# FF2 weight sums made in earlier stages and kept in HBM; 18 weight octets by seven products instead of 12

## The reference, cut to what matters

```python
x = x + jnp.einsum("bsd,de->bse", mixed, w_out[l])
h = _rmsnorm(x, ln2_w[l])
u = jax.nn.relu(jnp.einsum("bsd,df->bsf", h, w_ff1[l]))       # FF1: 256x2048 by 2048x8192
x = x + jnp.einsum("bsf,fd->bsd", jnp.square(u), w_ff2[l])    # FF2: 256x8192 by 8192x2048
```

## Time and profile before

| | value |
|---|---|
| median of the runs | 1516.24 us |
| profiled execution, its own time | 1515.4 us |
| its span | 1513.7 us |
| PE busy | 1503.6 us (99%), granted clock 1.0 all through |
| DVE busy | 1074.2 us (71%) |
| ACT busy | 783.6 us (52%) |
| GpSimd busy | 85.1 us (6%) |
| moved by DMA | 276.13 MB, mean 182 GB/s |

### The profile page before, as it was taken

The page is one execution under the profiler, slowest core; times in us unless marked ns, Lnnn a source line. Parts: engine busy times, 40 slices in busy tenths (PEclk is TensorE's granted clock), DMA queues, the critical chain, the costliest instruction groups (busy, mean ns, idle before and its releaser), DMA issues.

```text
span 1513.7 us, 19520 instructions
## 1 busy us (share of the span) xinstructions
PE 1503.6 (99%) x7508; PEld 1268.1 (84%) x7508; DVE 1074.2 (71%) x1274; ACT 783.6 (52%) x884; POOL 85.1 (6%) x121
## 2 busy tenths in 40 slices
PE   9999999999999999999999999999999999999999
PEld 6888888888888888888888888888888888888887
DVE  6866645778776877876655556688887566688976
ACT  6555444676654444544344545455544445455543
POOL 5000000000040100100000101100000101100000
PEclk9999999999999999999999999999999999999999
DMA  8565554454544444445655666656666665656662
GB/s 289 183 207 183 184 190 154 153 164 161 174 142 166 140 139 160 141 143 176 241 194 169 196 192 194 189 190 204 204 197 208 187 184 189 193 193 211 208 213 92
DMA packets 140295, 276.13 MB, mean 182 GB/s; under 512 B 7105, under 2 KB 7617, under 8 KB 139969
## 3 DMA queue, kind: packets, MB, share of 16 engines
q1 hardware_dynamic: 138960, 273.05, 55.0%
q10 hardware_dynamic: 1264, 2.13, 0.4%
HBM read 273.06 MB, written 2.10 MB: 182 GB/s over the span
## 4 chain that ended last, share of the span: by engine, by line
PE 95%; DVE 3%; issue 1%; ACT 0%; DMA 0%; SPq 0%; DVEq 0%; ACTq 0%
PE banks L493 43%; PE banks L852 16%; PE banks L920 14%; PE banks L855 8%; PE banks L898 8%; PE banks L509 2%; DVE lo L1404 1%; PE banks L758 1%; PE banks L633 1%; PE banks L606 1%; DVE diag L1423 1%; PE banks L749 1%; DMA x_tok<-in_x 0%; DVE both__111 L1423 0%; ACT hi L953 0%
## 5 line engine op out<-in xcount | busy, mean ns | idle before, releaser
L1404 DVE TENSOR_TENSOR lo<-raw,hi 128x1024 fp32r<-128x1024 f32 x384 | 472.6, 1235 | 317.3 <-ACT hi L953 313.9
L953 ACT ACTIVATE hi<-raw 128x1024 fp32r<-128x1024 f32 x383 | 404.7, 1058 | 439.6 <-PE banks L493 262.4
L493 PE MATMUL banks<-hi,st 128*128 128x512 f32 x1600 | 504.1, 396 | 2.2 <-DVE gates L1729 1.6
L493 PEld LDWEIGHTS banks<-hi,st 128*128 128x128 f32 x1600 | 292.5, 188 | 59.0 <-issue 2.3
L852 PE MATMUL banks<-st,hi 128*128 128x512 f32 x1024 | 321.6, 395 | 0.0
L493 PE MATMUL banks<-lo,st 128*128 128x512 f32 x800 | 312.2, 390 | 0.0
L855 PEld LDWEIGHTS banks<-st,lo 128*128 128x128 f32 x1024 | 192.4, 188 | 45.4
L855 PE MATMUL banks<-st,lo 128*128 128x256 f32 x1024 | 201.2, 278 | 0.0
L1354 ACT ACTIVATE hi<-raw 128x1024 fp32r<-128x1024 f32 x116 | 123.1, 1061 | 137.6 <-PE banks L920 115.3
L493 PEld LDWEIGHTS banks<-lo,st 128*128 128x128 f32 x800 | 150.2, 188 | 32.1
L1996 DVE TENSOR_TENSOR lo<-raw,hi 128x1024 fp32r<-128x1024 f32 x116 | 141.4, 1222 | 44.2 <-ACT hi L1354 41.7
(11 more groups left out here) (293 smaller groups left out, 1563.9 us busy)
## 6 DMA issues: line engine op xcount, KB each, us to landing
raw<-in_w_ff SPq DMA_DIRECT2D x128, 1024.0 KB, 5.2
raw<-in_w_in SPq DMA_DIRECT2D x99, 1024.0 KB, 5.0
raw<-in_w_out SPq DMA_DIRECT2D x16, 1024.0 KB, 5.3
raw<-in_w_gdn_proj SPq DMA_DIRECT2D x8, 1024.0 KB, 5.3
raw<-in_w_swa_proj SPq DMA_DIRECT2D x4, 1024.0 KB, 5.2
x_tok<-in_x SPq DMA_DIRECT2D x2, 1024.0 KB, 9.4
x<-in_x SPq DMA_DIRECT2D x1, 2048.0 KB, 7.7
raw<-in_w_in SPq DMA_DIRECT2D x2, 512.0 KB, 7.8
```

The source lines that it names most:

```text
L493: last = pe.matmul(acc[:, t], w[:, k0 + 2 * m + kk, P * t:P * t + P], v[:, (i + more) % PIECES, kk, :], start=m == 0 and kk == 0 and a == ...
L953: act.activation(hi[:, (i + more) % PIECES], raw[:, i // 2 % RAW, 2 * (i % 2):2 * (i % 2) + 2, :], ACT.Copy)\
L1404: dve.tensor_tensor(lo[:, (i + more) % PIECES], raw[:, i // 2 % RAW, 2 * (i % 2):2 * (i % 2) + 2, :], hi[:, (i + more) % PIECES].bitcast(F ...
```

## The change

The differences t1 to t4 are no longer made in FF2. In QKV, conv and FF1 SP loads FF2 weights as units (128 partitions x 2 rows x 1024 columns, 1 MB) into one of two buffers, DVE makes the four differences of the unit in place with three subtractions (one over 1024 columns a partition, two over 512), and SP stores the unit to a tensor `w_sums` outside the chip. A unit is half of what one octet in one pass needs. There are 16 units in QKV and conv (from step 12 on, one each five steps), which are those of half 0, and ten in each FF1 (from step 14, one each four and a half steps), which are those of half 1. SP issues the load five steps ahead and the store two steps behind.

In FF2 every piece is now a DMA of its own of 0.5 MB: b11, b21 and b22 from the weights, t1 to t4 from `w_sums`. SEVENS is now (0, 2, 3, 5) in half 0 and (0, 2, 3, 4, 5) in half 1, which is 18 octets of 32. Half 0 has 88 pieces and half 1 has 94, where each had 82. The buffers of the FF1 sums lie where `x1` is kept, so `x1` (2 MB) is stored to `x_kept` early in each FF1 and loaded back at piece 16 of each FF2. GpSimd makes the token sums of nine octets, not six. Some events were merged (a_t1 into a_t2, w_max into w_masked and so on), and SP's loops are now written out.

```diff
-SEVENS = (0, 3, 5)
+SEVENS = ((0, 2, 3, 5), (0, 2, 3, 4, 5))
+W_SUMS = [(half, np_, o, kk) for half in range(2) for np_ in range(2) for o in SEVENS[half] for kk in range(2)]
+SUM_STEPS = ([12 + 5 * n for n in range(4 * len(SEVENS[0]))], [14 + 9 * n // 2 for n in range(2 * len(SEVENS[1]))])
...
+            def product_piece(half, p, np_, o, n):
+
+                sp.wait_ge(lo_ready, piece0(half) + p - 2 * RAW + 1)
+                name = PRODUCTS[n] if o in SEVENS[half] else ("b11", "b21", "b12", "b22")[n]
...
+                sp.dma_start(raw_piece(p), src).then_inc(landed[p // 2 % RAW], 16)
+
+            def sums_in(part, n, h):
...
+                dst = (late_sum if part else early_sum)[h % 2]
...
+            def sums_out(part, h):
+                sp.wait_ge(ev["t_made"], 3 * h + 3)
+                sp.dma_start(w_sums[h], (late_sum if part else early_sum)[h % 2][:]).then_inc(ev[f"t_out{h % 2}"], 16)
+
+            def sums_traffic(part, at):
+
+                for s in (at - 1, at):
+                    for h, n in sums_now(part, s, 2):
+                        sums_out(part, h)
+                    for h, n in sums_now(part, s, -5):
+                        sums_in(part, n, h)
...
+            def keep_x(half):
...
+                sp.dma_start(x_kept, x1[:]).then_inc(ev["x_back"], 16)
...
+            def x_again(half):
...
+                sp.dma_start(x1[:], x_kept).then_inc(ev["x_back"], 16)
...
             def piece(half, p):
-                src, sem_, value = source(half, *pieces_of(half)[p])
-                act.wait_ge(sem_, value)
+                act.wait_ge(*tile_landed(half, p))
...
+            def weight_sums(part, at):
+
+                for h, _ in sums_now(part, at, 0):
+                    b = (late_sum if part else early_sum)[h % 2]
+                    dve.wait_ge(ev[f"t_in{h % 2}"], 16 * (h // 2) + 16)
+                    dve.tensor_tensor(b[:, 0].rearrange("p (c n) -> p c n", c=2), b[:, :, N:2 * N],
+                                      b[:, 0].rearrange("p (c n) -> p c n", c=2), ALU.subtract).then_inc(ev["t_made"], 1)
+                    dve.wait_ge(ev["t_made"], 3 * h + 1)
+                    dve.tensor_tensor(b[:, 1, N:2 * N], b[:, 1, N:2 * N], b[:, 0, 0:N], ALU.subtract)\
+                        .then_inc(ev["t_made"], 1)
+                for h, _ in sums_now(part, at, 1):
...
+                    dve.tensor_tensor(b[:, 1, 0:N], b[:, 1, 0:N], b[:, 1, N:2 * N], ALU.subtract)\
...
-            def weight_sums(half, np_, o):
...
-                return make(t1, b12, b11, 0), make(t2, b22, t1, 1), make(t3, b22, b12, 2), make(t4, b21, t2, 3)
```

More of the change, by code:

```diff
@@ L265, in piece0, with octet0, seven, raw_piece @@
             return 8 * (QG1 if half else QG0) + MORE_PIECES * half
[L267 to L271, removed]
+        def octet0(half, np_, o):
+            return HALF_PIECES[half] // 2 * np_ + sum(OCTET_PIECES[half][:o])
         def pieces_of(half):
[L274 to L285, removed]
+            return [(np_, o, n) for np_ in range(2) for o in range(OCTETS) for n in range(OCTET_PIECES[half][o])]
+        def seven(half, o):
+            return len(SEVENS[0]) * half + SEVENS[half].index(o)
+        def raw_piece(p):
+            return raw[:, p // 2 % RAW, 2 * (p % 2):2 * (p % 2) + 2, :]
+        def tile_landed(half, p):
+            tiles = QG0 + (MORE_LANDED + 16 if half else 0)
+            return landed[p // 2 % RAW], 16 * tiles + 32 * (p // 2 // RAW) + 32
+        def sums_now(part, at, after):
+            first = (0, len(SUM_STEPS[0]), len(SUM_STEPS[0]) + len(SUM_STEPS[1]))[part]
+            steps = SUM_STEPS[part > 0]
+            return [(first + n, n) for n, step in enumerate(steps) if step + after == at]
         def x1_part(np_, t, j):
@@ new lines, in sums_out, with quad_and_sums @@
+            def sums_out(part, h):
[7 more added lines that the diff above has]
+                        sums_in(part, n, h)
+            def quad_and_sums(part, g, q, w, k, c, first=False, more=0):
+                for j in range(4):
+                    tile(q, j, w, k + 4 * j, c, first, more)
+                    sums_traffic(part, 8 * (g - 1) - 3 + 2 * j)
@@ L361, in _ @@
                 quad(QE + i, w_o_v, 0, N * i)
[L362 to L372, removed]
+            for half, qf in enumerate((QF0, QF1)):
+                for g in range(8):
+                    quad_and_sums(1 + half, g, qf + g, w_1_v, 0, FF // 2 * half + N * g, more=MORE_PIECES * half)
+                    if g == 1:
+                        keep_x(half)
+                for p, (np_, o, n) in enumerate(pieces_of(half)):
+                    product_piece(half, p, np_, o, n)
+                    if p < 16 and p % 2:
+                        sums_traffic(1 + half, 52 + p)
+                    if p == 16:
+                        x_again(half)
         @block.gpsimd
@@ L469, in _ @@
             for half in range(2):
-                for k in range(len(SEVENS)):
-                    token_sums(half, k)
+                for o in SEVENS[half]:
+                    token_sums(half, o)
         @block.tensor
@@ L1385, in _ @@
                         u_hi_step(half, 7)()
-                    if o == SEVENS[-1] and n == 4:
+                    if o == SEVENS[half][-1] and n == 4:
                         copy_first(half, np_)
@@ L1630, in step @@
                 def step():
+                    if n == 0:
+                        for b in range(2):
+                            dve.wait_ge(ev[f"t_out{b}"], 8 * len(SUM_STEPS[0]))
                     tt_(gdn_qkv[:, n // 2, 4 * (n % 2):4 * (n % 2) + 4, :], y[:], e[:], ALU.mult,
```

258 lines of the change are left out of this document (130 added, 128 removed).

## The result

The changed kernel is slower: 1525.09 us (median of five, 1524.1 to 1525.85) against 1516.24, a ratio of 1.0059 (95% interval 1.0044 to 1.0073). The forecast of 1511.6 us, with a range to 1519, was wrong in sign.

What follows compares the result with a forecast made beforehand. PE was taken as the bound, busy 1503.6 of 1513.7 us, so matmul count and PE waits matter. -8.16 + 3.55 + 0 + 0 = -4.6 us gave 1511.6 us, range 1507.5 to 1519.

Steps and rivals of the forecast that it cites:

- Part 1: FF2: six more octets by seven products, 36 matmuls fewer on PE, gain 8.16 us.
- Part 2: QKV and conv: subtractions of 16 units delay PE at steps 17, 32 and 47 only, cost 3.55 us.
- Part 3: FF1: DVE's subtractions, ten units in each half, fit into 5.8 us of slack, cost 0.
- Part 4: DMA traffic in QKV, FF1 and FF2: rates of 387 to 392 GB/s just suffice and buffers absorb delays, cost 0.
- The rule of the Trainium skill: HBM side binds at about 358 GB/s: FF2 seven-product pieces would lose 13.1 us, making the sum +8.5 us.
- Part 5: The rest: SP's waits for stores, `keep_x`, extra FF2 pieces on ACT and DVE, and the tail, cost 0.
- rival C: FF1: DMA engines become the bound, 8 us lost in each half, 16 in all, 1527.6 us; chance 0.14.
- Rival A: QKV and conv: DVE's additions hide wholly, so only the 8.16 us gain counts, 1508.1 us; chance 0.16.
- B: More DVE places press on PE, above all in conv, or a unit loads late: 1513.4 to 1515.2 us; chance 0.14.
- D: FF2: seven-product octets go at DMA pace, 369 GB/s, buffers don't help, 7.6 us lost, 1519.2 us; chance 0.06.

Runs made afterwards that it cites:

- e7: Changed kernel with three unit buffers instead of two and unit loads issued seven steps ahead, not five: 1512.04 us, 0.9973 of the kernel before.
- e8: Changed kernel with three unit buffers, loads seven steps ahead, and the QKV and conv units moved to other steps: 1508.51 us, 0.9950 of the kernel before.
- e2: Changed kernel without the stores of the units made in FF1, loads and subtractions kept: 1514.43 us, 0.9992 of the kernel before.
- e3: Changed kernel without the subtractions in FF1, units still loaded and stored: 1514.75 us, 0.9992 of the kernel before.
- e4: Changed kernel with three unit buffers instead of two, loads still five steps ahead: 1518.68 us, 1.0017 of the kernel before.
- e9: Changed kernel with loads seven steps ahead, not five, still two unit buffers: 1534.55 us, 1.0129 of the kernel before.

## Why the prediction was wrong

**Part 1 (matmuls): right.** -2.7 and -5.4 us in FF2. The chain shows octets 2 to 5 of half 1 as one unbroken stretch of 4 x 9.52 us:

```profile
1369.31 10.88 PE banks L984 x48
1380.19 38.08 PE banks L962 x168
```

**Part 2 (QKV and conv): the mechanism right, the sum too small.** The transposes behind each rotary embedding show it group by group; before they are 22.68 us apart:

```profile
71.01 1.03 PE L574 MATMUL banks<-ident,t 128*128 128x128 f32 x8
94.90 1.09 PE L574 MATMUL banks<-ident,t 128*128 128x128 f32 x8
117.95 1.04 PE L574 MATMUL banks<-ident,t 128*128 128x128 f32 x8
142.37 1.09 PE L574 MATMUL banks<-ident,t 128*128 128x128 f32 x8
167.32 1.09 PE L574 MATMUL banks<-ident,t 128*128 128x128 f32 x8 [1.77 <-DVE t L1486]
```

The distances are 23.89, 23.05, 24.42 and 24.95, so +1.2 at step 17 (0.87 forecast), +0.4, +1.7 at step 32 (1.55 forecast), +2.3 in the last group, and some 1.0 behind it from step 47 (1.13 forecast in all for that step). In e7, whose units come in time, the same steps cost 1.1, 1.8 and 1.2 us, 4.3 in all up to FF1: near the 3.55. The other 2.3 us are units that came late, which Part 2 had at nothing. Most of it, 2.0 us, is the unit of step 47, behind whose subtractions the last `a_post` stood, as the chain of waits shows:

```profile
149.75 7.53 DMA early_sum<-in_w_ff
...
157.31 1.24 DVE early_sum L1529
...
160.40 1.13 DVE small L1596
...
166.04 1.23 DVE t L1486
```

The unit of step 37 was late as well (DVE waited 2.21 us for it), but the transposes behind it come 24.42 us after those before, and 24.44 in e7, so it cost PE nothing. With the places moved too (e8) 1.4 us remain, of which 0.8 is there already at the first transposes (49.1 us, 48.3 before).

**Part 3 (DVE work in FF1): right as far as it went.** e2 has every subtraction and loses nothing.

**Part 4 (DMA): right for FF2, and the rates were right.** The first and the last window of the stretch from 1381 to 1418 us have DVE busy for 8.92 of 10 and 6.17 of 7 us, PE without a gap, and 390 and 387 GB/s, beside the 385 that were worked out:

```profile
1381.00:1391.00 10.00, 10.00 (x46) 8.29 (x45) 8.92 (x9) 7.78 (x8) 0.00 (x0) 1.00 1.05 390
...
1411.00:1418.00 7.00, 7.00 (x33) 5.79 (x32) 6.17 (x7) 5.88 (x7) 0.00 (x0) 1.00 1.05 387
```

The landing of a 0.5 MB piece, estimated there at 3.9 us, was 6.0 (6.2 from `w_sums`), still inside the 8.4 us that the buffers give.

The rule of the Trainium skill ("DMA: Bandwidth & Descriptors", "Where 436 GB/s comes from") that was weighed there, some 358 GB/s from HBM for a core, is thus not what bound this lone core for these 37 us.

**Part 5 is the step that failed**, in the sentence that SP "may wait some 2 us, with 10 us and more of lead on the tiles behind it" and in the cost of 0 put on it. Of the 14.8 us between the forecast and the spans (-4.6 and +10.2), 11.7 are this step's and the rest is Part 2's. Part 5 took the landing of a lone 1 MB store (7.6 us) for a queue in which Part 4 itself wanted 359 of some 390 GB/s; it was 11.0, and SP waited 4.2 us each time (66.9 in 16). And it followed only the tiles behind the waiting SP, not the load of the next unit: that load was pushed behind the store, DVE reached the unit before it had landed, and DVE's queue held PE's `lo`. The window of five steps was counted at PE's pace (13.9 us, in rival C), while DVE takes its steps in bursts. e2 and e3 show that neither DVE's work without the stores nor the stores without DVE's work cost anything, e4 that freeing SP is not enough, e7 that the third buffer and two more steps of lead give back all 11.7 us, and e9 that the lead alone makes FF1 worse. Two stretches at half clock, one in each FF1, are part of these 11.7.

**Rival C** had the sign and the stage right, and its 8 us a half were near 5.1 and 6.6, but its mechanism was not the one: the DMA engines' rate wasn't the limit (e3, e7); their load made the landings long. **Rival A's** time was reached by e8, by moving what A said would hide. **B** named a late load of a unit, and priced it with its places at 1.8 to 3.6 us. **D** did not happen.

## What to carry to other kernels

Where a change adds a buffer that is loaded, worked on in place and stored, write down its whole cycle (load landing, work, store landing, with landings as they are in a full queue) and compare it with the time between two uses; with too few buffers it fails by latency while engines and bandwidth still have room. A wait for a DMA on an engine that works in order costs what stands behind it: place the operation where that engine has slack, and give the load a lead counted at the pace at which that engine catches up, not at the pace of the bottleneck. Before blaming bandwidth, leave out the work and keep the traffic.

## What the hardware showed that was not expected

A 1 MB load of a tile lands after 5.2 us in the kernel before, a unit of 1 MB in FF1 of e7 after 12.0 us, with the DMA engines at a share of 1.01 in the window shown, and FF1 takes no longer. A long landing is a sign of a queue, not of a loss. And PE's idle time seems to be charged twice: after a stretch in which it was busy for 1.91 of 4 us, its granted clock fell from 1.0 to 0.5 (2.4 to 1.2 GHz; the window from 942 to 946 us above shows the mean, 0.61) and came back after it. PE waited 2.62 us there, and 4 us at a mean of 0.61 lose some 1.6 us more (estimate), so the wait of DVE for one unit cost PE more than its length. That the idle time brought the clock down is argued from this order in time; no run tests it alone.
